# Gates and branch projections of a mix stage with tokens on partitions, and the merged result turned back by sixteen transposes

## What is computed

```python
h = rmsnorm(x, ln_mix[l])
z = h @ w_in[l]                                   # 1024 -> 512 + 512 + 128 + 128 + 2048
u_pool, q, k, v, gate_logits = jnp.split(z, splits, axis=-1)
a = pool_mixer(u_pool, pool_w[l], pool_scale[l]) @ w_pool_branch[l]      # 512 -> 1024
...
b = swa_sink_attention(q, k, v, sinks[l]) @ w_attn_branch[l]             # 512 -> 1024
g_pool, g_attn = jnp.split(jax.nn.sigmoid(gate_logits), 2, axis=-1)
x = x + (g_pool * a + g_attn * b) @ w_out[l]
```

## Time and profile before

| | before |
|---|---|
| median of 3 runs | 2067.92 us (2067.68 to 2068.56) |
| the profiled execution | 2069.39 us |
| its span | 2067.5 us |
| TensorE busy | 1748.4 us (85%) |
| VectorE busy | 1006.4 us (49%) |
| ScalarE busy | 700.4 us (34%) |
| GpSimd busy | 39.2 us (2%) |
| DMA, share of 16 engines | 75.7% |

### The profile page before, as it was taken

One profiled execution on the slowest core, in us unless ns is written; L12 is line 12 of the kernel. 1 busy time (PEld: TensorE's weight loads), 2 busy tenths in 40 slices (PEclk: granted clock), 3 DMA queues, 4 the chain that ended last, 5 costly groups with the idle time before them and its releaser, 6 DMA issues.

```text
span 2067.5 us, 27842 instructions
## 1 busy us (share of the span) xinstructions
PE 1748.4 (85%) x12122; PEld 1342.2 (65%) x12124; DVE 1006.4 (49%) x1385; ACT 700.4 (34%) x1036; POOL 39.2 (2%) x46
## 2 busy tenths in 40 slices
PE   9986655566998755556599999999999999999999
PEld 7943321222795321222268889998888888999888
DVE  5722110110672110011068778877777667787666
ACT  6310000000651000000055555655546445465453
POOL 0000000000000000000000003000000000300000
PEclk9998877888999988888799999999999999999999
DMA  9899999999989999999985554545555556445552
GB/s 400 340 423 430 430 430 430 431 430 425 399 333 416 430 431 431 430 430 430 417 333 195 192 210 174 181 171 184 184 205 194 191 183 215 176 160 184 185 196 88
DMA packets 65072, 626.37 MB, mean 303 GB/s; under 512 B 7216, under 2 KB 7344, under 8 KB 14512
## 3 DMA queue, kind: packets, MB, share of 16 engines
q1 hardware_dynamic: 64944, 624.50, 75.7%
HBM read 623.42 MB, written 1.05 MB: 302 GB/s over the span
## 4 chain that ended last, share of the span: by engine, by line
PE 71%; DMA 22%; DVE 3%; ACT 1%; SPq 1%; issue 1%; DVEq 0%; ACTq 0%
PE ps L610 14%; PE ps L614 7%; PE ps L554 6%; PE ps L556 6%; PE ps L555 6%; PE ps L905 5%; DMA dense_ring<-in_moe_w_down 5%; PE ps L911 4%; DMA expert_ring_a<-in_moe_w_down 4%; PE ps L1137 4%; PE ps L1159 4%; DMA expert_ring_a<-in_moe_w_up 3%; DMA expert_ring_b<-in_moe_w_gate 3%; PE ps L1143 2%; PE ps L1164 2%; PE ps L873 2%
## 5 line engine op out<-in xcount | busy, mean ns | idle before, releaser
L1746 DVE TENSOR_TENSOR w_lo<-dense_ring,w_hi 128x1024 fp32r<-128x1024 f32 x397 | 467.7, 1221 | 54.8 <-ACT w_hi L1313 53.3
L1313 ACT CAST w_hi<-dense_ring 128x1024 fp32r<-128x1024 f32 x397 | 395.7, 1048 | 47.6 <-PE ps L556 26.1
L610 PE MATMUL ps<-h_both,w_hi 128*128 128x512 f32 x1344 | 321.6, 391 | 0.9 <-DVE work L2240 0.9
L610 PEld LDWEIGHTS ps<-h_both,w_hi 128*128 128x128 f32 x1344 | 247.0, 188 | 50.3 <-DVE work L2240 2.3
L905 PE MATMUL ps<-expert_ring_b,work 128*32 128x512 f32 x576 | 148.2, 682 | 73.3 <-DMA expert_ring_a<-in_moe_w_up 61.2
L554 PE MATMUL ps<-h_both,w_hi 128*128 128x256 f32 x656 | 188.5, 287 | 0.4 <-DVE h_both L1752 0.3
L2130 DVE TENSOR_TENSOR work<-work,ps 128x512 f32<-128x512 f32 x14 | 9.6, 688 | 362.4 <-PE ps L905 362.4
L556 PE MATMUL ps<-h_both,w_lo 128*128 128x256 f32 x656 | 185.6, 283 | 0.0
L555 PE MATMUL ps<-h_both,w_hi 128*128 128x256 f32 x656 | 185.6, 283 | 0.0
L905 PE MATMUL ps<-dense_ring,work 128*32 128x512 f32 x528 | 147.6, 611 | 36.9 <-DMA expert_ring_b<-in_moe_w_up 28.1
L614 PEld LDWEIGHTS ps<-h_both,w_lo 128*128 128x128 f32 x1344 | 172.3, 191 | 6.6
(11 more groups left out here) (343 smaller groups left out, 2966.1 us busy)
## 6 DMA issues: line engine op xcount, KB each, us to landing
dense_ring<-in_dense SPq DMA_DIRECT2D x207, 1024.0 KB, 4.8
expert_ring_b<-in_moe_w_up SPq DMA_DIRECT2D x28, 2048.0 KB, 34.9
dense_ring<-in_moe_w_gate SPq DMA_DIRECT2D x27, 2048.0 KB, 34.8
expert_ring_a<-in_moe_w_down SPq DMA_DIRECT2D x23, 2048.0 KB, 35.2
expert_ring_a<-in_moe_w_up SPq DMA_DIRECT2D x18, 2048.0 KB, 32.5
expert_ring_b<-in_moe_w_gate SPq DMA_DIRECT2D x12, 2048.0 KB, 34.4
dense_ring<-in_moe_w_down SPq DMA_DIRECT2D x11, 2048.0 KB, 31.6
expert_ring_a<-in_moe_w_gate SPq DMA_DIRECT2D x9, 2048.0 KB, 20.9
```

The source lines that it names most:

```text
L610: mm(bank[b + f], w[0][:, f, k, :], h_pairs[:, k, :], start=k == 0, stop=False)
L1313: S.copy(half_of(key, f, 0), tile_of(slot(key), key, f)).then_inc(rounded.up(key, f), 1)
L1746: V.tensor_tensor(half_of(key, f, 1), tile_of(slot(key), key, f), half_of(key, f, 0).bitcast(F32), ALU.subtract).then_inc(remainder.up(key ...
```

## The change

- The eight gate chunks are laid out as four pairs: each chunk holds 512 gate columns of one half of the 1024 input features. `gate_products` works like `wide_products`: h is stationary, 512 columns move, 24 matmuls a chunk, and a pair of chunks fills bank 6 with tokens 0 to 127 and bank 7 with the others.
- ScalarE takes the tanh straight out of PSUM, with half the token's factor as scale (`half_token`, one small operation on VectorE). VectorE's eight scalings go.
- A branch piece is now 512 output features of 128 tokens, 12 matmuls with the activations stationary. `merge` works on [128 tokens, 512 features].
- The merged result must have features on partitions for the output. Behind all branch pieces stand four groups of four transposes into banks 0, 5, 6 and 7; ScalarE writes the high part out of PSUM, and VectorE, behind all merges, the low part.
- The split of chunk 14 goes to an earlier place on ScalarE and between the merges on VectorE. The first output chunk waits for groups 0 and 1 (k below 4) and then for groups 2 and 3.

```diff
 E_ROWS = -(-N_F // KD)
+GATES = range(5, 13)
 LAST_OF_FFN = [("e", 0), ("e", 1), ("d", N_GRP // 2), ("e", 2), ("e", 3), ("e", 4), ("e", 5)]
...
             chunks += [((s, j), wide("w_in_2", l, 2 * CHUNK, j), True) for j in range(2)]
-            chunks += [((s, 2 + j), cols("w_in_2", l, c * CHUNK), True) for j, c in enumerate([4, 0, 1] + list(range(5, 13)))]
+            chunks += [((s, 2 + j), cols("w_in_2", l, c * CHUNK), True) for j, c in enumerate([4, 0, 1])]
+            chunks += [((s, j), wide("w_in_2", l, (j - (j - 5) % 2) * CHUNK, (j - 5) % 2), True) for j in GATES]
             chunks.append(((s, "pool_w"), heads_of("pool_w_2", l), False))
...
     rinv, _ = place("rinv", T + 8)
-    root_inverse, rinv, of_token = rinv, rinv[:, 0:T], rinv[:, T:T + TT]
+    root_inverse, rinv, of_token, half_token = rinv, rinv[:, 0:T], rinv[:, T:T + TT], rinv[:, T + TT:T + 2 * TT]
     both = [place(n, KD)[0] for n in ("gain_both", "gain_squared")]
...
     qkT = k_view(heads[:, TT * U * HD:], T)
-    merged = heads[:, 0:KD * T].rearrange("p (k t) -> p k t", k=KD)
+    merged = heads[:, 0:TT * D].rearrange("p (a d) -> p a d", a=TT)
     windows = wk(3 * 4 * L, scratch)
...
     pT = windows[:, 0:N_Q * 3 * P]
-    sig = k_view(wk(16 * T, scratch), T)
+    sig = wk(TT * 2 * D, scratch).rearrange("p (a d) -> p a d", a=TT)
     assert at[0] <= SCRATCH_F
...
-        return key[1] in ("d", "wp", "wa") or key[0] in AS_COLUMNS and key[1] in (0, 1)
+        return key[1] in ("d", "wp", "wa") or key[0] in AS_COLUMNS and key[1] in (0, 1) or is_gate(key)
+    def is_gate(key):
+        return key[0] in ("m0", "m1") and key[1] in GATES
...
         return b.rearrange("p (f t) -> p f t", f=2)
+    def block_of(m, i):
+        c, tt = divmod(i, 2)
+        return m[:, 4 * c:4 * c + 4, tt * P:(tt + 1) * P]
...
     BRANCH_BANK = ((2, 3, 0, 1), (4, 5, 6, 7))
+    Y_BANK = (0, 5, 6, 7)
...
                     ins = triple(bank[b + tt], [h[:, kd, tt * P:(tt + 1) * P] for h in h_halves],
+                                 [v[:, k, :] for v in w], kd == 0, kd == KD - 1)
+                ins.then_inc(products.up(key, tt), 1)
+        def gate_products(key, s):
+            w = [k_view(m, 2 * CHUNK) for m in w_halves[halves_of[key]]]
+            pair_of, half = divmod(key[1] - 5, 2)
+            for tt in range(TT):
+                if half == 0:
+                    claim(6 + tt, acted, "sig", s, pair_of, tt)
+                for k in range(KD // 2):
+                    kd = half * KD // 2 + k
+                    PE.wait_ge(remainder, key, k // 2)
+                    PE.wait_ge(remainder, "h", s, kd)
+                    ins = triple(bank[6 + tt], [h[:, kd, tt * P:(tt + 1) * P] for h in h_halves],
                                  [v[:, k, :] for v in w], kd == 0, kd == KD - 1)
...
                     token_products((s, j), b, s)
+                elif j < 5:
+                    claim(b, vec, "u", s, j)
+                    tile_products((s, j), b, h_of(s))
                 else:
-                    claim(b, vec, *(("u", s, j) if j < 5 else ("scaled", s, j)))
-                    tile_products((s, j), b, h_of(s))
+                    gate_products((s, j), s)
                 if j == 7:
...
             PE.wait_ge(remainder, "oT", s, 1)
+            for i in range(3):
+                branch(s, 1, i)
+            branch(s, 1, 3)
             for i in range(4):
-                branch(s, 1, i)
-            project(s, 13, lambda k: (remainder, "merged", s, k // 2), x=y_halves)
+                turned(s, i)
+            project(s, 13, lambda k: (remainder, "merged", s, 2 * (k // 4) + 1), x=y_halves)
+        def turned(s, i):
+            c, tt = divmod(i, 2)
+            PE.wait_ge(vec, "merged", s, i)
+            claim(Y_BANK[i], remainder, "merged", s, i)
+            for q in range(4):
+                ins = TE.transpose(bank[Y_BANK[i]][:, q * P:(q + 1) * P], merged[:, tt, (4 * c + q) * P:(4 * c + q + 1) * P], C("ident"))
+            ins.then_inc(products.up("turned", s, i), 1)
...
             name, x = (("wp", poolY), ("wa", oT))[br]
-            c, q = divmod(i, 2)
+            c, tt = divmod(i, 2)
             key = (s, name, c)
...
             claim(b, vec, "merge", s, br, i)
-            for f in range(2):
-                for k in range(4):
-                    ins = triple(bank[b][:, f * T:(f + 1) * T], [v[:, k, (2 * q + f) * P:(2 * q + f + 1) * P] for v in w],
-                                 [v[:, k, :] for v in x], k == 0, k == 3)
+            for k in range(4):
+                ins = triple(bank[b], [v[:, k, tt * P:(tt + 1) * P] for v in x], [v[:, k, :] for v in w], k == 0, k == 3)
             ins.then_inc(products.up("branch", s, br, i), 1)
...
-        if by_rows(key) and key[1] in (0, 1) or key[0][0] == "m" and key[1] == 2:
+        if by_rows(key) and key[1] in (0, 1) or key[0][0] == "m" and key[1] == 2 or is_gate(key):
             return key, 1
...
+        def tanh_of(s, pair_of):
+            ACT.wait_ge(vec, "half_token", s)
+            for tt in range(TT):
+                ACT.wait_ge(products, (s, 6 + 2 * pair_of), tt)
+                S.activation(sig[:, tt, pair_of * 2 * CHUNK:(pair_of + 1) * 2 * CHUNK], bank[6 + tt], ACTF.Tanh,
+                             scale=half_token[:, tt:tt + 1]).then_inc(acted.up("sig", s, pair_of, tt), 1)
         def mix(l):
...
                 if j == 10:
+                    tanh_of(s, 2)
                     for b in range(2):
...
                                        acted.up("qkT", s, tt, j0), 1)
-                if j >= 5:
-                    c = 2 * (j - 5)
-                    ACT.wait_ge(vec, "scaled", s, j)
-                    S.activation(sig[:, c:c + 2, :], sig[:, c:c + 2, :], ACTF.Tanh, scale=0.5).then_inc(acted.up("sig", s, j), 1)
+                if j in (6, 8, 12):
+                    tanh_of(s, (j - 6) // 2)
                 if j == 3:
...
             hi((s, 13))
-            for q in range(4):
-                if q == 2:
-                    hi((s, 14))
-                ACT.wait_ge(vec, "merged", s, q)
-                S.copy(pair(y_halves[0], q), pair(merged, q)).then_inc(rounded.up("merged", s, q), 1)
+            hi((s, 14))
+            for i in range(4):
+                ACT.wait_ge(products, "turned", s, i)
+                S.copy(block_of(y_halves[0], i), k_view(bank[Y_BANK[i]], P)).then_inc(rounded.up("merged", s, i), 1)
             project(s, 13, [(s, 15), (s, 16), (f"f2{l}", "g", 0)])
...
         def merge(s, br, i):
-            b, k0 = BRANCH_BANK[br][i], 2 * i
+            c, tt = divmod(i, 2)
+            gate = sig[:, tt, br * D + c * 2 * CHUNK:br * D + (c + 1) * 2 * CHUNK]
+            m = merged[:, tt, c * 2 * CHUNK:(c + 1) * 2 * CHUNK]
             DVE.wait_ge(products, "branch", s, br, i)
-            DVE.wait_ge(acted, "sig", s, 12)
-            dst = merged[:, k0:k0 + 2, :] if br == 0 else sig[:, 8 + k0:8 + k0 + 2, :]
-            seq(V.scalar_tensor_tensor(dst, sig[:, br * 8 + k0:br * 8 + k0 + 2, :], 1.0, two(bank[b]), ALU.add, ALU.mult),
+            DVE.wait_ge(acted, "sig", s, 2 * br + c, tt)
+            seq(V.scalar_tensor_tensor(gate if br else m, gate, 1.0, bank[BRANCH_BANK[br][i]], ALU.add, ALU.mult),
                 "merge", s, br, i)
             if br == 1:
-                m = merged[:, k0:k0 + 2, :]
-                V.tensor_tensor(m, m, dst, ALU.add).then_inc(vec.up("merged", s, i), 1)
-                lo_pair(("merged", s, i), y_halves, merged, i)
+                V.tensor_tensor(m, m, gate, ALU.add).then_inc(vec.up("merged", s, i), 1)
+        def y_lo(s, i):
+            DVE.wait_ge(rounded, "merged", s, i)
+            V.tensor_tensor(block_of(y_halves[1], i), k_view(bank[Y_BANK[i]], P), block_of(y_halves[0], i).bitcast(F32),
+                            ALU.subtract).then_inc(remainder.up("merged", s, i), 1)
...
                     reciprocal_later(s)
+                    seq(V.tensor_scalar(half_token, of_token, 0.5, None, ALU.mult), "half_token", s)
                 elif 3 <= j < 5:
...
                         vec.up("u", s, j), 1)
-                elif j >= 5:
-                    b, c = 6 + j % 2, 2 * (j - 5)
-                    DVE.wait_ge(products, (s, j), 1)
-                    V.tensor_tensor(sig[:, c:c + 2, :], two(bank[b]), over_tiles(rinv), ALU.mult).then_inc(
-                        vec.up("scaled", s, j), 1)
                 if 3 <= j < 6:
...
             lo((s, 13))
+            merge(s, 1, 0)
+            merge(s, 1, 1)
+            lo((s, 14))
+            merge(s, 1, 2)
+            merge(s, 1, 3)
             for i in range(4):
-                merge(s, 1, i)
-            lo((s, 14))
+                y_lo(s, i)
             project(s, 13, [(s, 15), (s, 16), (f"f2{l}", "g", 0)], 0.5)
```

## The result

| | before | changed |
|---|---|---|
| median | 2068.57 us (8 runs, 2067.44 to 2071.92) | 2074.49 us (8 runs, 2072.97 to 2076.30) |
| ratio, with its 95% interval | | 1.0027 [1.0018, 1.0035] |
| the profiled execution | 2069.39 us | 2076.30 us |
| its span | 2067.5 us | 2074.4 us |

The change makes the kernel slower by 0.27%. The forecast was 2072.0 us, in a range of 2068.5 to 2076.0.

What follows compares the result with a forecast made beforehand. TensorE's queue bounds the mix stages. Terms -3.86 + 1.17 + 1.73 + 1.69 + 0.39 + 0.93 = +2.05 us a stage, +4.1 in all on a 2067.92 median: 2072.0 us, range 2068.5 to 2076.0.

Steps and rivals of the forecast that it cites:

- signs that the prediction named for being wrong: In the changed profile: expected idle stretches absent, a fourth one there, or wide matmuls at another pace than 0.227 us.
- What bounds it: Mix stages m0 and m1: TensorE's own queue sets the end, so any wait reaching it is paid in full.
- Fewer and wider matmuls: Gates and branches: 288 pairs of 256-column matmuls become 512-column ones, each saving 0.0134 us, -3.86 us a stage.
- The two bank waits: TensorE waits for VectorE's copy before chunk 5, +1.17 us, and for ScalarE's tanh behind the softmax before chunk 11, +1.73.
- Transposes: Behind the branch pieces: sixteen new transposes on TensorE at 0.106 us each, +1.69 us a stage.
- The tail: After the last branch piece: TensorE waits for the last merge, +0.39 us, and for y_lo with a restart, +0.93.
- Bank waits that do not reach TensorE (1): Chunk 11: tanh done before TensorE asks, 2068.5 us; with chunk 5's wait away too, 2066.2. Not slower, chance 0.22.
- an unseen wait (2): Another wait or a longer link, such as a weight half or slower y_lo: 2074 to 2076 us, chance 0.14.
- a falling clock (3): Granted clock falls in the new gaps, some 1.5 us lost at one fall a stage: 2075 us, chance 0.07.
- wide matmuls or transposes that run one behind the other (4): TensorE overlaps new work less: wide matmuls without saving, 2079.7 us, or transposes at 0.34 each, 2079.5; chance 0.04.
- all waits absent (5): All three waits missing: -2.17 us a stage, 2063.6 us, faster by over 0.2%; chance 0.04.
- The prediction's own case: Whole kernel: the summed terms hold, 2071 to 2073.5 us, on both sides of the 0.2% line; chance 0.49.

## Why the prediction was right, and the term that was mis-sized

The forecast of +2.05 us a stage was measured as +2.57; the sign, the places and the count of the waits were right. One of the signs that the prediction named for being wrong did come: wide matmuls with another pace, 48 of the 288. Cut at starts that both traces have, the stage's difference falls into six stretches. The rows are those of the earlier trace rows, of the earlier trace rows and of the two sections above; in the fourth and fifth column stands what the two traces give:

| stretch of stage m0 | forecast | measured | before | changed |
|---|---|---|---|---|
| stage's start to chunk 5 (the bank) | +1.05 | +1.05 | 1240.30 to 1270.75 | 1242.13 to 1273.63 |
| chunk 5 to first branch matmul (restart, 192 pairs, the tanh) | 0.12 - 2.57 + 1.73 = -0.72 | -0.75 | to 1322.96 | to 1325.09 |
| branch pieces of poolY, 48 pairs | -0.64 | -0.53 | to 1340.31 | to 1341.91 |
| branch pieces of oT, 48 pairs | -0.64 | -0.23 | to 1351.70 | to 1353.07 |
| transposes and waits of the tail | 1.69 + 0.39 + 0.81 = +2.89 | +2.95 | none | to 1356.02 |
| output chunks (restart) | +0.12 | +0.08 | to 1374.69 | to 1379.09 |
| sum | +2.06 | +2.57 | | |

- **What bounds it** held: at granted clock 1.00 and with no gap, TensorE's queue was the stage, and each wait taken out gave back its full length on the program's stage (1.17, 1.76).
- **Fewer and wider matmuls.** The failing step is "that is the form that the change gives to gates and branches, in the same stage and with the same kinds of operands": both durations were taken from products over h, and the 0.16 a branch piece that followed from them was mis-sized. For the gates it was true. For oT neither duration fits: its old matmuls were the faster ones (0.1186) and its new ones the slower (0.2326). The first was in the trace of the kernel before and could have been read: 96 matmuls of oT between two rows. The second was not there. Of the error of 0.52, 0.41 are this. 0.11 are poolY's pieces, where three of the four average 0.2290: they come behind a break, and the 0.2266 was read far from one (from the seventh of 48 on).
- **The two bank waits** held to 0.05, including the softmax chain of seven links, forecast to end at 1312.30 and found at 1312.24. A sum over queued instructions works when each link's distance of starts is a row.
- **Transposes** held: the 24 of the probabilities still take 2.54 us in the changed kernel, and in the tail they start 0.109 apart. The Trainium skill's page "TensorE: Matmul & The Clock Gate" (PE-mode transpose) has about 275 ns for one, and taken as a pace that would have made the stage an estimated 2.7 us longer than it is. The trace agrees with the figure as the length of one record, 0.272 us; such records overlap, and the prediction priced by the distance of starts.
- **The tail** held to 0.06, restart of the output chunk included.
- **Rivals.** Bank waits that do not reach TensorE (1), an unseen wait (2), a falling clock (3), wide matmuls or transposes that run one behind the other (4), and all waits absent (5): none happened. The prediction's own case ended at 2073.5, and 2074.49 lies above it, in the 2074 to 2076 that it gave to rival 2. That rival's cause, a further or a longer wait, isn't there: the pace of oT and the executions' spread took its place. So the range held the result in part by luck.
- **Median.** The forecast added 4.1 us to a median of 2067.92. The runs beside the changed kernel had 2068.57; with 5.14 from the stages that gives 2073.7, and 2074.49 was measured. The rest of 0.8 lies within the spread of the first half.
